# Passes of the expert value products reordered: by PSUM bank instead of by pass

## The chip, the cores and the metric

The kernel runs on one core of one Trainium2 chip. The metric is the device time of one execution in microseconds (us); lower is better. TensorE's clock has two levels here, 1.2 and 2.4 GHz; the profile shows the granted clock as a share of the higher one.

## The reference

One transformer-like layer (gated delta rule, mLSTM, a feed-forward part and a per-layer-embedding gate) is followed by a second block with two layers: an RG-LRU mixer and a forgetting-attention mixer, each followed by a PEER expert layer. There are 256 tokens (T) of width 1024 (D), all in float32. The change lies in the PEER layers:

```python
def retrieve_chunk(xc):
    ...
    expert = e1 * PEER_KEYS + e2
    g = jax.nn.softmax(top_s, axis=-1)
    u = jnp.take(expert_u, expert, axis=0)
    act = jax.nn.gelu(jnp.einsum('thkd,td->thk', u, xc).astype(jnp.float32), approximate=False)
    w = (g * act).astype(xc.dtype)
    return jnp.einsum('thk,thkd->td', w, jnp.take(expert_v, expert, axis=0))
```

There are 16384 experts, 128 x 128 keys. The kernel does not gather. It multiplies all experts and weights the unchosen ones with zero.

## The kernel before, in words

**Tiles.** Every weight matrix is streamed from HBM in tiles of 128 partitions x 1024 float32 (512 KB), through `ring`, which has 4 slots (`RAW`). SyncE issues these loads. A PEER layer (`experts(L)`, L = 0 and 1) streams 128 tiles of `expert_u` and then 128 tiles of `expert_v`, one tile for each first key.

**Three passes.** A float32 product is made of fp32r products. Each tile is cut into a high part (`high`, ScalarE, line 1645) and a low part, the tile minus its high part (`low`). GpSimd makes the low part of `expert_u` tiles (line 1766) and VectorE that of `expert_v` tiles (`values_low`, line 2312). Both `high` and `low` have 3 slots (`CUT`). The activations are cut likewise. A product is then high x high, high x low of the activations, and low x high: three passes, numbered 0, 1 and 2, and only pass 2 reads `low`.

**Stage hidden.** `hidden(s_)` multiplies one `expert_u` tile with the activations, 24 matmuls of 256 columns (3 passes x 8, line 1216), all into one bank of the PSUM tensor `mm`. Tile s_ takes bank s_ % 4. ScalarE applies gelu, VectorE weights the result (`weigh_hidden`, line 2295) into `placed`. Between hidden tiles stand the `place` groups (line 1237), which place the routing weights.

**Stage values.** `values(s_)` multiplies one `expert_v` tile (moving operand, two halves of 512 columns) with the weighted activations `wts` (stationary operand, 128 x 128, for the two token tiles c = 0 and 1). The four pairs of c and half have the four banks of the PSUM tensor `ms`, and each bank accumulates over all 128 tiles. A tile is 12 matmuls (line 1256). `wts` has 3 slots: its high part comes from ScalarE (`weights_high`, line 1674), its low part from VectorE (`weights_low`, line 2303), which raises `weighted`. In layer 0 the ring also carries 48 tiles of modulation weights during this stage, which VectorE adds up (lines 2325 and 2328).

**What sets the order.** Each engine's instructions stand in an order written out by hand, and semaphores join them. On TensorE `values(s_)` waits for `weighted` and `high_done`, and, ahead of its pass 2, for `low_done` (`low_ready(q)`, line 771). When its last matmul ends it raises `tiles_used`, which frees the slot of `high`, `low` and `wts` for the tile three later: ScalarE's cut of the high part waits for it. A slot of `ring` is freed by `low_done`. On VectorE the last hidden tile is weighted, then `weights_low` is made for the last slot, and then come `values_low(0)`, `(1)`, `(2)` and so on:

```python
for s_ in range(KEYS):
    values_low(s_)
    if s_ >= CUT:
        weights_low(s_)
```

After the 128th tile of a layer the four banks are copied out, turned by TensorE (line 1283) and added to `x`.

Of the kernel before, what the change touches and what calls it, by code (L numbers as in the profile page):

```python
# [31 lines left out]
TT = T // P  # L32
# [8 lines left out]
CUT = 3  # L41
# [389 lines left out]
def build(nc, streams, xT, pT, consts, vecs, small_w, fox_f_w, lru_gate_w, out):  # L431
    with ExitStack() as ctx:
        sem = Signals(nc, ctx)

        def sb(name, shape, dt=F32):
            return ctx.enter_context(nc.sbuf_tensor(name, shape, dt))
# [4 lines left out]
        high = sb("high", [P, CUT, SLOT], F32R)  # L441
        low = sb("low", [P, CUT, SLOT], F32R)
# [309 lines left out]
        def _(pe):  # L752
# [11 lines left out]
            def parts_of(name, i, width=SLOT):  # L764

                q = CUT0[name] + i
                pe.wait_ge(sem("high_done"), q + 1)
                return q, high[:, q % CUT, 0:width], low[:, q % CUT, 0:width]

            def low_ready(q):  # L770

                pe.wait_ge(sem("low_done"), q + 1)
# [176 lines left out]
            for u in range(8):  # L949
                hd, c = u // 2, u % 2  # L950
# [6 lines left out]
            for u in range(8):  # L957
                hd, c = u // 2, u % 2
# [14 lines left out]
            for u in range(8):  # L973
                hd, c = u // 2, u % 2
# [5 lines left out]
            for u in range(8):  # L980
                hd, c = u % 4, u // 4
# [119 lines left out]
            q, wh, wl = parts_of("w_out", 0)  # L1101
# [18 lines left out]
            for m in range(KD):  # L1120
                dst = bank(OUT0["ffn_down"] + m)[:, 0:T]
                k0 = 0
                for i, rows in enumerate(DOWN):
                    q, wh, wl = parts_of("ffn_down", 3 * m + i)
# [29 lines left out]
            for j in range(RT):  # L1154
                for b, kind in enumerate(("x", "g")):
                    q, wh, wl = parts_of("lru_in", 2 * j + b)
# [13 lines left out]
            for i, (m, half) in enumerate(LRU_OUT):  # L1170
# [3 lines left out]
                q, wh, wl = parts_of("lru_out", i)  # L1174
# [10 lines left out]
            def experts(L):  # L1185
# [56 lines left out]
                def values(s_):  # L1242

                    q = q0 + KEYS + s_
                    pe.wait_ge(sem("weighted"), KEYS * L + s_ + 1)
                    pe.wait_ge(sem("high_done"), q + 1)
                    if s_ == 0:
                        pe.wait_ge(sem("place_copied"), GROUPS * (L + 1))
                        pe.wait_ge(sem("place_weighed"), GROUPS * (L + 1))
                    for pass_, (a_, b_) in enumerate(((0, 0), (0, 1), (1, 0))):  # L1250
                        if pass_ == 2:
                            low_ready(q)
                        v_ = (high, low)[a_][:, q % CUT, :]
                        for c in range(TT):
                            for half in range(2):
                                ins_ = pe.matmul(ms[:, 2 * c + half, :], wts[:, s_ % 3, b_, c * P:(c + 1) * P],  # L1256
                                                 v_[:, half * 512:(half + 1) * 512], start=s_ == 0 and pass_ == 0,
                                                 stop=s_ == KEYS - 1 and pass_ == 2, skip_group_check=True)
                    ins_.then_inc(sem("tiles_used"), 1)
# [8 lines left out]
                for s_ in range(KEYS):  # L1268
                    values(s_)
                    if L == 0 and s_ in LATE_SUMS_AFTER:  # L1270
                        if s_ == LATE_SUMS_AFTER[0]:
                            pe.wait_ge(sem("hidden_weighed"), KEYS - FIRST_MIXED)
                        sum_late_mods([LATE_SUMS_AFTER.index(s_)], mm[:, 3])
# [3 lines left out]
                for b in range(4):  # L1277

                    c, half = b % 2, b // 2
# [1376 lines left out]
```

## Time and profile before

| | us |
|---|---|
| time, median of 3 runs | 2575.62 |
| lowest and highest run | 2573.45, 2577.27 |
| profiled execution, span from first to last instruction | 2581.3 |
| TensorE busy in it | 2480.5 (96%) |
| VectorE, ScalarE, GpSimd busy | 1757.1, 1224.5, 1210.8 |

The profiled execution's own device time is not listed beside its span; its span lies 5.7 us above the median of the runs. All times are us from the span's start. "PE" is TensorE's matmuls and "PEld" its weight loads; DVE is VectorE, ACT ScalarE, POOL GpSimd, SPq the DMA queue of SyncE. Matmuls are pipelined: a matmul starts while the one before it is still draining, so the time that a matmul takes of the engine is the distance between two starts, and not the mean duration of the row. The "chain" of the profile page is followed back from the last instruction through what released each step.

### The profile page before, as it was taken

What the parts mean: (1) busy time and instruction counts of PE and PEld (TensorE: products, weight loads), DVE (VectorE), ACT (ScalarE), POOL (GpSimd) and SP (SyncE); (2) the same over time, 40 slices, a digit from 0 to 9 for tenths busy, and PEclk for the clock granted to TensorE, in tenths of its full rate; (3) what the DMA queues carried; (4) which work ended last, traced back from release to release, by engine and by line L of the source; (5) the groups of instructions that cost most, each with busy time, mean ns of one, the idle gap of its engine ahead of it and who ended that gap; (6) DMA issues with size and microseconds to landing.
All of it is one profiled execution on the core that took longest, in us unless ns stands there. A gap on an engine that the chain in (4) does not pass through costs nothing.

```text
span 2581.3 us, 46939 instructions
## 1 busy us (share of the span) xinstructions
PE 2480.5 (96%) x18074; PEld 2294.0 (89%) x18074; DVE 1757.1 (68%) x3289; ACT 1224.5 (47%) x2091; POOL 1210.8 (47%) x506
## 2 busy tenths in 40 slices
PE   7899899979799999999999999999999999999999
PEld 6899899969789999998888888888999999888887
DVE  4558553367719979997776764651897999655555
ACT  5325433446445544444444444544555444445453
POOL 4437577645468987771000004446798777200000
PEclk8899899989899999999999998998999999999999
DMA  4325576754255655556777772334565445566664
GB/s 161 98 74 168 202 256 233 278 205 123 82 164 180 191 178 156 156 156 222 254 255 260 252 240 92 108 97 152 174 192 183 154 160 156 173 195 189 194 189 146
DMA packets 125918, 457.93 MB, mean 177 GB/s; under 512 B 13968, under 2 KB 15376, under 8 KB 125584
## 3 DMA queue, kind: packets, MB, share of 16 engines
q1 hardware_dynamic: 125424, 450.73, 54.5%
q10 hardware_dynamic: 288, 4.33, 0.4%
q8 instruction: 145, 2.38, 0.4%
q14 instruction: 61, 0.50, 0.1%
HBM read 453.95 MB, written 1.05 MB: 176 GB/s over the span
## 4 chain that ended last, share of the span: by engine, by line
PE 86%; DVE 7%; ACT 3%; issue 2%; DMA 1%; POOL 1%; SPq 0%; DVEq 0%; POOLq 0%; ACTq 0%
PE mm L1216 27%; PE ms L1256 27%; PE mm L786 20%; PE ms L1237 3%; PE ms L793 1%; DMA ring<-w_ple_gate 1%; DVE hs L1805 1%; PE mm L793 1%; PE mm L801 1%; DVE work L1805 1%; PE mm L899 1%; POOL low L1766 1%; DVE scratch L1805 1%; DVE work L2494 1%; DVE work L1799 0%
## 5 line engine op out<-in xcount | busy, mean ns | idle before, releaser
L1766 POOL TENSOR_TENSOR low<-ring,high 128x1024 fp32r<-128x1024 f32 (+2 forms) x502 | 1210.6, 2424 | 1004.4 <-ACT high L1438 847.2
L1645 ACT ACTIVATE high<-ring 128x1024 fp32r<-128x1024 f32 x506 | 536.3, 1060 | 356.4 <-PE ms L1256 320.3
L1216 PE MATMUL mm<-hs,high 128*128 128x256 f32 x4096 | 520.4, 280 | 3.4 <-ACT high L1438 3.4
L1256 PE MATMUL ms<-high,wts 128*128 128x512 f32 x2048 | 511.2, 392 | 0.0
L1216 PEld LDWEIGHTS mm<-hs,high 128*128 128x128 f32 x4096 | 486.8, 188 | 3.8 <-issue 3.8
L2312 DVE TENSOR_TENSOR low<-ring,high 128x1024 fp32r<-128x1024 f32 x256 | 313.5, 1226 | 248.3 <-ACT high L1645 248.0
L1256 PEld LDWEIGHTS ms<-high,wts 128*128 128x128 f32 x2048 | 384.2, 188 | 83.3
L786 PE MATMUL mm<-hs,high 128*128 128x256 f32 x2608 | 346.4, 287 | 4.8 <-DVE parts L1799 4.6
L1438 ACT ACTIVATE high<-ring 128x1024 fp32r<-128x1024 f32 (+2 forms) x252 | 258.1, 1031 | 185.4 <-PE mm L786 114.4
L786 PEld LDWEIGHTS mm<-hs,high 128*128 128x128 f32 x2608 | 326.0, 196 | 9.3 <-issue 7.7
L1256 PE MATMUL ms<-low,wts 128*128 128x512 f32 x1024 | 275.7, 391 | 3.0 <-DVE low L2312 3.0
L1216 PE MATMUL mm<-hs,low 128*128 128x256 f32 x2048 | 274.0, 276 | 0.5 <-POOL low L1766 0.5
L1216 PEld LDWEIGHTS mm<-hs,low 128*128 128x128 f32 x2048 | 251.1, 188 | 0.9 <-POOL low L1766 0.9
L1256 PEld LDWEIGHTS ms<-low,wts 128*128 128x128 f32 x1024 | 192.1, 188 | 46.2 <-DVE low L2312 3.8
L786 PE MATMUL mm<-hs,low 128*128 128x256 f32 x1304 | 178.1, 279 | 0.4 <-POOL low L1766 0.4
L1653 ACT ACTIVATE mm<-mm 128x256 f32<-128x256 f32 (+47 forms) x148 | 39.7, 268 | 269.8 <-PE mm L1216 269.8
L786 PEld LDWEIGHTS mm<-hs,low 128*128 128x128 f32 x1304 | 163.6, 191 | 0.7 <-POOL low L1766 0.6
L2277 DVE TENSOR_TENSOR onehots<-onehots,ms 128x512 bf16<-128x512 bf16 x256 | 163.3, 679 | 0.0
L1447 ACT ACTIVATE work<-mm 128x256 f32<-128x256 f32 (+2 forms) x145 | 60.2, 417 | 205.6 <-PE mm L786 168.2
L1655 ACT ACTIVATE work<-mm 128x256 f32<-128x256 f32 (+17 forms) x248 | 79.9, 322 | 137.1 <-PE mm L1216 137.1
L786 PE MATMUL mm<-parts,high 128*128 128x256 f32 x896 | 126.9, 294 | 15.7 <-DVE parts L1799 10.2
L786 PEld LDWEIGHTS mm<-parts,high 128*128 128x128 f32 x896 | 117.1, 199 | 18.4 <-DVE parts L1799 10.7
(315 smaller groups left out, 2802.3 us busy)
## 6 DMA issues: line engine op xcount, KB each, us to landing
ring<-w_peer_experts SPq DMA_DIRECT2D x512, 512.0 KB, 3.7
work<-w_mod SPq DMA_DIRECT2D x48, 512.0 KB, 4.5
ring<-w_late_mods SPq DMA_DIRECT2D x48, 512.0 KB, 4.6
ring<-w_ffn_up SPq DMA_DIRECT2D x44, 512.0 KB, 3.7
ring<-w_peer_q SPq DMA_DIRECT2D x32, 512.0 KB, 3.6
ring<-w_fox_in SPq DMA_DIRECT2D x32, 512.0 KB, 3.6
ring<-w_lru_in SPq DMA_DIRECT2D x22, 512.0 KB, 3.5
ring<-w_gates SPq DMA_DIRECT2D x16, 512.0 KB, 3.6
```

The lines of the kernel that those rows point to most:

```text
L786: ins = pe.matmul(dst, l, r_, start=first and s_ == 0 and k == 0, stop=last and s_ == 2 and k == rows - 1, skip_group_check=True)
L1216: ins_ = pe.matmul(mm[:, s_ % BANKS, 0:T], w_[:, k * P:(k + 1) * P], hs[:, b_, k, :], start=pass_ == 0 and k == 0, stop=pass_ == 2 and k = ...
L1237: ins_ = pe.matmul(ms[:, 2 + i % 2, t * P:(t + 1) * P], onehot[:, i % 2, 3, t, :], onehot[:, i % 2, third, t, :], start=third == 0, stop=t ...
L1256: ins_ = pe.matmul(ms[:, 2 * c + half, :], wts[:, s_ % 3, b_, c * P:(c + 1) * P], v_[:, half * 512:(half + 1) * 512], start=s_ == 0 and pa ...
L1438: act.activation(high[0:rows, q % CUT, 0:width], ring[0:rows, n_ % RAW, 0:width], ACT.Copy) \
L1447: S.did(act.activation(dst, src, func), taken(n))
L1645: act.activation(high[:, (q0 + i) % CUT, :], ring[:, n_ % RAW, :], ACT.Copy) \
L1655: ins = act.activation(placed[:, s_, at:T], src[:, at:T], ACT.Gelu)
L1766: pool.tensor_tensor(low[0:rows, cut_slot, 0:width], ring[0:rows, raw_slot, 0:width], high[0:rows, cut_slot, 0:width].bitcast(F32), ALU.su ...
L1805: S.did(dve.scalar_tensor_tensor(out=out_, in0=a, scalar=s, in1=b, op0=op0, op1=op1, **kw), name)
L2277: dve.tensor_tensor(onehot[:, k % 2, s], onehot[:, k % 2, 2], third(s), ALU.mult)
L2312: dve.tensor_tensor(low[:, q % CUT, :], ring[:, n % RAW, :], high[:, q % CUT, :].bitcast(F32), ALU.subtract).then_inc(sem("low_done"), 1)
```

## The change

`low_ready(q)` is called ahead of the tile's first matmul, and the loops are turned inside out. Before, a pass went over all four banks and then the next pass did; now each bank gets its three passes, one behind the other. The 12 matmuls of a tile, their operands, and the flags `start` and `stop` of each are the same, and so are all other engines' instructions (one line of code fewer moves the line numbers behind it by one).

```diff
-                    for pass_, (a_, b_) in enumerate(((0, 0), (0, 1), (1, 0))):
-                        if pass_ == 2:
-                            low_ready(q)
-                        v_ = (high, low)[a_][:, q % CUT, :]
-                        for c in range(TT):
-                            for half in range(2):
+                    low_ready(q)
+                    for c in range(TT):
+                        for half in range(2):
+                            for pass_, (a_, b_) in enumerate(((0, 0), (0, 1), (1, 0))):
+                                v_ = (high, low)[a_][:, q % CUT, :]
                                 ins_ = pe.matmul(ms[:, 2 * c + half, :], wts[:, s_ % 3, b_, c * P:(c + 1) * P],
                                                  v_[:, half * 512:(half + 1) * 512], start=s_ == 0 and pass_ == 0,
                                                  stop=s_ == KEYS - 1 and pass_ == 2, skip_group_check=True)
```

TensorE, from the end of the last hidden tile of layer 0 into value tile 0, before (output, then operands, then partitions x columns):

```order
L1216 MATMUL mm<-hs,low 128x256 [waits low_done]
L1216 MATMUL mm<-hs,low 128x256 x7
L1256 MATMUL ms<-high,wts 128x512 [waits place_copied,place_weighed,high_done,weighted]
L1256 MATMUL ms<-high,wts 128x512 x7
L1256 MATMUL ms<-low,wts 128x512 [waits low_done]
L1256 MATMUL ms<-low,wts 128x512 x3
L1256 MATMUL ms<-high,wts 128x512 [waits high_done,weighted]
```

The same place after the change:

```order
L1216 MATMUL mm<-hs,low 128x256 [waits low_done]
L1216 MATMUL mm<-hs,low 128x256 x7
L1255 MATMUL ms<-high,wts 128x512 [waits place_weighed,place_copied,low_done,high_done,weighted]
L1255 MATMUL ms<-high,wts 128x512
L1255 MATMUL ms<-low,wts 128x512
L1255 MATMUL ms<-high,wts 128x512 x2
L1255 MATMUL ms<-low,wts 128x512
L1255 MATMUL ms<-high,wts 128x512 x2
L1255 MATMUL ms<-low,wts 128x512
L1255 MATMUL ms<-high,wts 128x512 x2
L1255 MATMUL ms<-low,wts 128x512
L1255 MATMUL ms<-high,wts 128x512 [waits low_done,high_done,weighted]
```

The wait for the low part has moved over eight matmuls, from the ninth to the first, and now joins the others there.

TensorE, a later value tile of layer 0 (tile 1), before:

```order
L1256 MATMUL ms<-high,wts 128x512 [waits high_done,weighted]
L1256 MATMUL ms<-high,wts 128x512 x7
L1256 MATMUL ms<-low,wts 128x512 [waits low_done]
L1256 MATMUL ms<-low,wts 128x512 x3
L1256 MATMUL ms<-high,wts 128x512 [waits high_done,weighted]
```

And after the change:

```order
L1255 MATMUL ms<-high,wts 128x512 [waits low_done,high_done,weighted]
L1255 MATMUL ms<-high,wts 128x512
L1255 MATMUL ms<-low,wts 128x512
L1255 MATMUL ms<-high,wts 128x512 x2
L1255 MATMUL ms<-low,wts 128x512
L1255 MATMUL ms<-high,wts 128x512 x2
L1255 MATMUL ms<-low,wts 128x512
L1255 MATMUL ms<-high,wts 128x512 x2
L1255 MATMUL ms<-low,wts 128x512
L1255 MATMUL ms<-high,wts 128x512 [waits low_done,high_done,weighted]
```

In every tile the low products now stand third, sixth, ninth and twelfth, and a tile has one place to wait instead of two.

## Rows read from the trace of the kernel before

**Rows 1.** Page, part 4: the chain that ended last, shares of the span by line
```profile
PE mm L1216 27%; PE ms L1256 27%; PE mm L786 20%; PE ms L1237 3%; PE ms L793 1%; DMA ring<-w_ple_gate 1%; DVE hs L1805 1%; PE mm L793 1%; PE mm L801 1%; DVE work L1805 1%; PE mm L899 1%; POOL low L1766 1%; DVE scratch L1805 1%; DVE work L2494 1%; DVE work L1799 0%
```

**Rows 2.** Page, part 5: matmul groups of the value products; count, busy, mean ns, idle
```profile
L1256 PE MATMUL ms<-high,wts 128*128 128x512 f32 x2048 | 511.2, 392 | 0.0
...
L1256 PE MATMUL ms<-low,wts 128*128 128x512 f32 x1024 | 275.7, 391 | 3.0 <-DVE low L2312 3.0
```

**Rows 3.** Timeline, TensorE, value tile 0 of layer 0: start, us, count, idle before
```profile
1182.38 2.00 PE L1256 MATMUL ms<-high,wts 128*128 128x512 f32 x8
1185.86 1.19 PE L1256 MATMUL ms<-low,wts 128*128 128x512 f32 x4 [1.49 <-DVE low L2312]
1186.89 2.00 PE L1256 MATMUL ms<-high,wts 128*128 128x512 f32 x8
```

**Rows 4.** Timeline, ScalarE and VectorE in that stretch, and VectorE's cut of tile 3
```profile
1183.81 0.41 ACT L1674 ACTIVATE wts<-work 128x256 fp32r<-128x256 f32 x1
1184.25 0.42 DVE L2303 TENSOR_TENSOR wts<-work,wts 128x256 fp32r<-128x256 f32 x1 [0.77 <-ACT wts L1674]
1184.59 3.49 DVE L2312 TENSOR_TENSOR low<-ring,high 128x1024 fp32r<-128x1024 f32 x3
...
1190.57 1.23 DVE L2312 TENSOR_TENSOR low<-ring,high 128x1024 fp32r<-128x1024 f32 x1 [1.82 <-ACT high L1645]
```

**Rows 5.** Timeline, TensorE, value tile 0 of layer 1
```profile
2219.58 2.00 PE L1256 MATMUL ms<-high,wts 128*128 128x512 f32 x8
...
2223.06 1.19 PE L1256 MATMUL ms<-low,wts 128*128 128x512 f32 x4 [1.48 <-DVE low L2312]
```

**Rows 6.** Timeline, layer 1: the parts of value tile 3, and its start
```profile
2225.45 1.23 DVE L2312 TENSOR_TENSOR low<-ring,high 128x1024 fp32r<-128x1024 f32 x1 [0.16 <-ACT high L1645]
...
2226.59 0.42 DVE L2303 TENSOR_TENSOR wts<-work,wts 128x256 fp32r<-128x256 f32 x1
...
2229.58 2.00 PE L1256 MATMUL ms<-high,wts 128*128 128x512 f32 x8
```

**Rows 7.** Timeline, TensorE, from hidden tile to hidden tile
```profile
1176.03 1.07 PE L1216 MATMUL mm<-hs,low 128*128 128x256 f32 x8
1176.94 1.98 PE L1216 MATMUL mm<-hs,high 128*128 128x256 f32 x16
1178.75 1.07 PE L1216 MATMUL mm<-hs,low 128*128 128x256 f32 x8
```

**Rows 8.** Windows: busy (count) by engine, granted clock, DMA share, GB/s
```profile
336.00:341.00 5.00, 5.00 (x24) 5.00 (x25) 3.33 (x5) 1.11 (x2) 2.38 (x1) 0.50 0.60 205
...
693.50:696.90 3.40, 3.40 (x19) 3.40 (x18) 0.00 (x0) 0.88 (x3) 3.06 (x2) 0.50 0.35 110
...
1182.00:1190.00 8.00, 6.51 (x31) 5.13 (x31) 4.92 (x6) 2.16 (x4) 0.00 (x0) 1.00 0.38 121
...
2224.00:2572.00 348.00, 348.00 (x1522) 285.51 (x1521) 196.59 (x252) 170.57 (x250) 0.00 (x0) 1.00 0.60 188
```

**Rows 9.** Timeline, TensorE, behind an idle stretch of 4.58 us
```profile
335.90 3.75 PE L786 MATMUL mm<-hs,high 128*128 128x256 f32 x16 [4.58 <-DVE parts L1799]
339.45 1.91 PE L786 MATMUL mm<-hs,low 128*128 128x256 f32 x8
341.15 2.36 PE L786 MATMUL mm<-hs,high 128*128 128x256 f32 x16
343.35 1.07 PE L786 MATMUL mm<-hs,low 128*128 128x256 f32 x8
```

**Rows 10.** Timeline, TensorE, behind an idle stretch of 2.53 us
```profile
692.21 2.69 PE L786 MATMUL mm<-parts,high 128*128 128x256 f32 x16 [2.53 <-DVE x L1805]
694.70 1.91 PE L786 MATMUL mm<-parts,low 128*128 128x256 f32 x8
696.41 1.10 PE L786 MATMUL mm<-parts,high 128*128 128x256 f32 x6
697.35 0.52 PE L786 MATMUL mm<-parts,low 128*128 128x256 f32 x3
```

## The prediction

> **What bounds the kernel now.** I read the page first: the chain that ended last runs over TensorE, with 27% of the span in the value products and 27% in the hidden ones [rows 1]. So a nanosecond saved or lost on each value matmul counts in full, and so does a microsecond in which TensorE stands still in that stage. The groups by line then give the size of the stage and its one fault: 2048 + 1024 = 3072 matmuls, with 3.0 us idle ahead of the low products, released by VectorE's cut of the low part [rows 2]. The timeline finds the 3.0 us: 1.49 us in tile 0 of layer 0 [rows 3] and 1.48 us in tile 0 of layer 1 [rows 5]. Everywhere else the stage is dense: from 2224 to 2572 us TensorE is busy for the whole 348 us, with 1522 matmuls and the clock at its upper level [rows 8], which is 348 / 1522 = 228.7 ns from start to start. The row's mean duration of 392 ns is not what a matmul takes of the engine.
>
> **The change, part by part.** The 3072 matmuls and as many weight loads stay. Two things move: the wait for the low part, eight matmuls forward, and the order of the banks.
>
> *The wait, in the steady state: nothing.* For tile 3 of layer 1 the low part is ready at 2225.45 + 1.23 = 2226.68, and the low part of `wts`, for which the tile's first matmul waits in any case, only at 2226.59 + 0.42 = 2227.01; the tile starts at 2229.58 [rows 6]. The new wait thus ends 0.33 us ahead of one that stands there already, and 2.9 us ahead of its use. What hides it is the tile that runs meanwhile, 12 x 0.229 = 2.75 us. If that cover were gone, the price would be the 1.83 us of the eight matmuls, in each of 256 tiles, but nothing here takes it away: ScalarE starts to cut a tile when the tile three before it is done, and has two tiles' time. Layer 0 is tighter, as the ring also carries the modulation tiles: its tile 3 has its low part at 1190.57 + 1.23 = 1191.80 [rows 4] and starts at 1186.89 + 2 x 2.75 = 1192.39, 0.6 us later. That still suffices, and the later start of tile 0 (below) adds 1.8 us to it.
>
> *The wait, in tile 0 of each layer: 1.83 us.* In layer 0 the low part is made from 1184.59 on, behind the last `wts` parts on ScalarE and VectorE (to 1184.22 and 1184.67) [rows 4]; they come from the last hidden tile, and nothing of that chain depends on a value product. So it is ready at the same moment as before, and TensorE resumes at 1185.86 [rows 3]. Before, eight matmuls had run by then (from 1182.38 on) and four were left. Now all twelve are left. The eight cost 8 x 228.7 ns = 1.83 us on the chain. Layer 1 shows the same stretch: start at 2219.58, resumed at 2223.06 [rows 5]. Two layers: 2 x 1.83 = 3.7 us. It is not won back, since the stage behind is bound by TensorE itself. Tiles 1 and 2 are not late: VectorE makes three low parts in one stretch of 3.49 us, the last ready at 1188.1 [rows 4], and tile 1 now starts at 1186.89 + 1.83 = 1188.7. Queued behind the waiting TensorE is only its own stream; ScalarE's cut for tile 3 waits for the end of tile 0, and moves by 1.8 us along with it, within the 2.9 us of slack.
>
> *The clock behind the longer gap: 2.3 us a layer.* Now TensorE has no matmul between the last hidden one and the resumption. A group of eight such matmuls is busy for 0.16 us beyond the start of the next group (1176.03 + 1.07 against 1176.94) [rows 7], so the last hidden one ends at 1182.38 + 0.16 = 1182.54, and the idle stretch is 1185.86 - 1182.54 = 3.3 us, where it was 1.49. The stretch of 1.49 us left the clock at 1.00 [rows 8]. How a longer one is answered, two places show. Behind 2.53 us idle the clock fell to 0.50 (1.2 GHz) from 693.5 to 696.9 [rows 8], and 16 + 8 + 6 = 30 matmuls took 697.35 - 692.21 = 5.14 us [rows 10]; at 0.113 us each, the distance at the upper level [rows 7], they take 3.40. That is 1.7 us lost. Behind 4.58 us idle it was 0.50 as well [rows 8], and 40 matmuls took 343.35 - 335.90 = 7.45 us in place of 4.53 [rows 9], 2.9 us lost. My 3.3 us lies between these two, so I take the middle, 2.3 us, with 1.7 and 2.9 as ends, and zero as the outer bound if the clock doesn't fall. Two layers: 4.6 us.
>
> *The order of the banks: nothing.* Before, every value matmul went to another bank than the one ahead of it; now only four of twelve do. The trace has no value matmul that stays in its bank. The nearest rows are the hidden tiles, which stay in one bank for 24 matmuls and then change it. The eight low matmuls that end a tile, the change of bank, of tile and of pass included, take 1176.94 - 1176.03 = 0.91 us, or 114 ns each, and the 16 within a tile 1178.75 - 1176.94 = 1.81 us, or 113 ns each [rows 7]. So neither staying nor changing has a price at 256 columns, within the 10 ns to which the rows are given. I take zero for 512 columns. The bounds: in its own bank a 256-column matmul takes 113.3 ns for 256 columns, which is 226.7 ns for 512, and the value matmul takes 228.7. If the whole difference of 2.0 ns came from changing banks, 8 x 256 = 2048 matmuls would give back 4.1 us. The other bound: 113.3 ns is 6.6 ns above the 106.7 ns that 256 columns take at 2.4 GHz, and 228.7 is 15.4 ns above 213.3 ns; if 6.6 ns is fixed and the other 8.8 ns is the bank, 2048 x 8.8 ns = 18.0 us. I stay near zero since rows 7 see the very event and show no price. Upwards I allow 2 ns as well (+4.1 us), as staying in a bank might cost what changing does.
>
> *Weight loads: nothing.* The old order used each stationary tile twice in a row, the new one changes it at nearly every matmul. Each matmul has its own load in both, and the loads lie beside the matmuls: busy 285.51 of 348 us with no matmul idle [rows 8].
>
> **The sum.** 3.7 + 4.6 = 8.3 us. Against the profiled execution: 2581.3 + 8.3 = 2589.6. That execution's span lies 5.7 us above the median of the runs, 2575.6, and the difference carries over: 2575.6 + 8.3 = 2583.9 us, 0.32% slower. About 0.2%, 5.2 us, is what a measurement of this kernel can tell from no change.
>
> **The rivals.**
> 1. *The clock holds in both layers.* Then 3.7 us remain: 2579.3, within 0.2%. For it: 1.49 us idle did nothing. Against it: the idle stretch of 2.53 us did. If it falls in one layer alone, it is 3.7 + 2.3 = 6.0, 2581.6 us, just on the slower side.
> 2. *Changing banks had a price at 512 columns, and TensorE gets faster.* Its place is the steady state of both value stages. Each nanosecond is worth 2.05 us, so 4.1 ns pays for the sum, and 6.6 ns makes the kernel faster by over 0.2%. With the 8.8 ns from above it is 2575.6 + 8.3 - 18.0 = 2565.9 us. For it: 15.4 ns above the column time want an explanation. Against it: rows 7, and the clock at 1.00 and no idle through the 348 us [rows 8].
> The Trainium skill's page "TensorE: Matmul & The Clock Gate", section "A second HAM failure mode: psum-queue depth-cycling", speaks for this rival: it tells of a kernel with 512-column matmuls which lost throughput as it cycled through the banks, with TensorE idle between groups and its clock swinging. The trace disagrees, as there is neither idle time nor a lower clock to give back here. The same page, "Back-to-back issue gap", gives about 216 ns for an isolated 512-column matmul; as an estimate by that figure, a value matmul freed of all its surplus over it would give 2048 x 12.7 ns = 26 us, more than my bound from rows.
> 3. *Staying in a bank costs.* A write that must add to what the one just before it left may have to wait. At 5 ns that is 10 us more, 2594 us. Against it: the hidden tiles do just this, at 113 ns.
> 4. *The change does nothing that counts.* The low part might come earlier by some freed time elsewhere, and the order of TensorE's stream is certain. That leaves 2575.6. I see no engine that gets anything freed ahead of tile 0.
>
> **How the numbers follow.** Forecast (clock falls in both layers, banks free): 0.60. One layer alone: 0.12. Clock holds: 0.11. Banks gain: 0.08, of which half ends within 0.2% (the small bound: 8.3 - 4.1 = +4.2) and half faster. Staying costs: 0.04. Nothing: 0.05. Slower by over 0.2% are the forecast, the costly bank and most of the one-layer case (0.04 of its 0.12 falls back within the measurement's spread): 0.60 + 0.04 + 0.08 = 0.72, less 0.03 for runs that come out low, 0.69. Faster: 0.04, and 0.01 of spread, 0.05. Within 0.2%: the rest, 0.26. The range: its upper end is the sum with both clocks at their end, 3.7 + 5.8 = 9.5, and half the spread of the runs, 1.9, so 2587; its lower end the clock that holds, 2579.3, less the same 1.9 and rounded down, 2577. Left out are the banks' large gain, the costly bank and nothing at all, under 2 in 10.
>
> **What would show it.** Idle time ahead of the value matmuls of about 3.3 us twice, in the first tile, released by VectorE's low part, and none elsewhere. A granted clock of 0.50 in the microseconds behind 1186 and 2225. Tile 1 1.8 us later against the last hidden matmul, and more with the clock. From there on 228.7 ns from start to start and 2.75 us a tile. If that distance is another one, the bank step is wrong; if the low wait shows in later tiles, the slack is; if the clock stays at 1.00, the clock step is.

## The result and the profile after

| | before | after |
|---|---|---|
| time, median of 4 runs, us | 2576.11 | 2592.45 |
| lowest and highest run, us | 2573.45, 2577.27 | 2587.87, 2599.67 |
| ratio, 95% interval | | 1.0053 [1.0036, 1.0069] |
| profiled execution, span, us | 2581.3 | 2597.9 |

The changed kernel is slower, by 16.3 us in this comparison. 8.3 were forecast, and 2592.45 lies above the range, which ended at 2587.0. Three of the four runs of the kernel before are the three from which the forecast was made. The profiled execution of the changed kernel took 2599.67 us, 1.8 us more than its span of 2597.9.

The page of the changed kernel, part 4 (shares of the span by line) and the groups of the value products in part 5, which answer to [rows 1, 2]:

```profile
PE ms L1255 27%; PE mm L1216 27%; PE mm L786 20%; PE ms L1237 3%; PE ms L793 1%; DMA ring<-w_ple_gate 1%; PE mm L793 1%; DVE hs L1804 1%; DVE work L1804 1%; PE mm L899 1%; PE mm L801 1%; POOL low L1765 1%; DVE scratch L1804 1%; DVE work L2493 1%; DVE work L1798 0%
...
L1255 PE MATMUL ms<-high,wts 128*128 128x512 f32 x2048 | 638.4, 393 | 6.8 <-DVE low L2311 6.8
...
L1255 PE MATMUL ms<-low,wts 128*128 128x512 f32 x1024 | 404.3, 395 | 0.0
```

The idle time has grown from 3.0 to 6.8 us, has moved from the low products to the high ones, and is still released by VectorE's low part. The busy times of the two groups (511.2 and 275.7 us before) look 256 us larger. That is no loss: since high and low products now alternate, each group also counts the time in which the other one's pipelined matmul is draining. The counts of matmuls in fixed windows tell better. Here are the changed kernel's (busy and count by engine, then granted clock, DMA share, GB/s):

```profile
1193.00:1200.00 7.00, 6.29 (x15) 4.97 (x16) 3.50 (x4) 0.74 (x1) 0.00 (x0) 0.51 0.75 239
1203.00:1210.00 7.00, 7.00 (x32) 5.73 (x31) 5.35 (x6) 3.48 (x6) 0.00 (x0) 1.00 0.63 193
2234.00:2241.00 7.00, 5.82 (x14) 4.59 (x15) 3.30 (x3) 0.27 (x1) 0.00 (x0) 0.51 0.61 208
2260.00:2560.00 300.00, 300.00 (x1313) 246.14 (x1312) 170.26 (x219) 149.52 (x219) 0.00 (x0) 1.00 0.62 191
```

From 2260 to 2560 us 1313 value matmuls ran, as against 1312 in the same 300 us of the kernel before:

```profile
2260.00:2560.00 300.00, 300.00 (x1312) 246.15 (x1311) 170.31 (x218) 149.29 (x219) 0.00 (x0) 1.00 0.62 191
```

So the order of the banks changed nothing there. What did change is at the start of each value stage, where the clock stands at half (0.51 is a window that lies almost wholly at 1.2 GHz). Layer 0, TensorE, in the changed kernel (start, us, count, idle before), which answers to [rows 3]:

```profile
1189.23 1.07 PE L1216 MATMUL mm<-hs,low 128*128 128x256 f32 x8
1193.71 1.19 PE L1255 MATMUL ms<-high,wts 128*128 128x512 f32 x2 [3.41 <-DVE low L2311]
1194.70 0.63 PE L1255 MATMUL ms<-low,wts 128*128 128x512 f32 x1
1195.12 1.05 PE L1255 MATMUL ms<-high,wts 128*128 128x512 f32 x2
...
1198.96 1.03 PE L1255 MATMUL ms<-high,wts 128*128 128x512 f32 x2
```

TensorE stands idle for 3.41 us. Then a bank's three matmuls take 1195.12 - 1193.71 = 1.41 us, 0.43 to 0.56 us each, and the twelve of tile 0 take 1198.96 - 1193.71 = 5.25 us, where 2.75 was the time at the upper clock. From the last hidden matmul to the last value matmul of the stage it took 365.15 us in layer 0 and 357.76 in layer 1, read off the starts in the timeline; before, it was 360.44 and 353.22. That is 4.71 + 4.54 = 9.25 us in the places which the change touches. The two spans differ by 16.6 us. The other 7.3 us lie in code that the change leaves alone. They lie ahead of the first value tile, which starts 11.3 us later (1193.71 against 1182.38), 3.6 of them by its own wait.

### The profile page after: what moved, and what is told of

Same layout as the page of the kernel before. It is cut to its first block, busy times and chain, and to the rows that moved or that the text cites. A ratio compares the mean times of both kernels' runs of the same rounds, so it can differ in the third digit from the quotient of the medians.

```text
span 2597.9 us, 46939 instructions
## 1 busy us (share of the span) xinstructions
PE 2492.5 (96%) x18074; PEld 2305.9 (89%) x18074; DVE 1750.2 (67%) x3289; ACT 1225.0 (47%) x2091; POOL 1210.6 (47%) x506
## 4 chain that ended last, share of the span: by engine, by line
PE 86%; DVE 7%; ACT 3%; issue 2%; DMA 1%; POOL 1%; SPq 0%; DVEq 0%; POOLq 0%; ACTq 0%
PE ms L1255 27%; PE mm L1216 27%; PE mm L786 20%; PE ms L1237 3%; PE ms L793 1%; DMA ring<-w_ple_gate 1%; PE mm L793 1%; DVE hs L1804 1%; DVE work L1804 1%; PE mm L899 1%; PE mm L801 1%; POOL low L1765 1%; DVE scratch L1804 1%; DVE work L2493 1%; DVE work L1798 0%
## 5 line engine op out<-in xcount | busy, mean ns | idle before, releaser
L1255 PE MATMUL ms<-high,wts 128*128 128x512 f32 x2048 | 638.4, 393 | 6.8 <-DVE low L2311 6.8
L1255 PE MATMUL ms<-low,wts 128*128 128x512 f32 x1024 | 404.3, 395 | 0.0
```

## The experiments

### The same kernels again, and each half of the change alone

The first four ran together. Two are unchanged copies. The third moves the wait alone:

```diff
+                    low_ready(q)
                     for pass_, (a_, b_) in enumerate(((0, 0), (0, 1), (1, 0))):
-                        if pass_ == 2:
-                            low_ready(q)
                         v_ = (high, low)[a_][:, q % CUT, :]
```

The fourth has the order by banks in every tile but the first of each layer:

```diff
+                    if s_ == 0:
+                        for pass_, (a_, b_) in enumerate(((0, 0), (0, 1), (1, 0))):
+                            if pass_ == 2:
+                                low_ready(q)
...
+                    else:
+                        low_ready(q)
+                        for c in range(TT):
+                            for half in range(2):
+                                for pass_, (a_, b_) in enumerate(((0, 0), (0, 1), (1, 0))):
...
```

> The kernel before, unchanged, as a control: 2576 us in every theory, within 0.1% of its own runs. What it tells is the spread: in the profiled executions the 256-column matmuls stand at either of two distances at the upper clock, 113.3 or 117.8 ns, for stretches of tens to hundreds of us (the profile of before has 11 us above 113.3 ns in all, that of after 21 us). Theory LUCK: the level is drawn anew in each execution, so the control has executions with 15 to 20 us of it too, and single runs 5 us or more above the others. Theory PROGRAM: the level depends on the program, and the control repeats 2573 to 2578 us.

> The changed kernel again, in more rounds. Theory START (the longer wait in tile 0 of each layer and the half clock behind it, 3.95 to 4.6 us a layer in the traces): 9 us over before, 2585 us, and the rest of the 16 us was chance. Theory PROGRAM or BANK: 2592 us again, 16 us over before, and the 7 us more lie outside tile 0 of the layers.

> Only the wait for the low part is moved ahead of the tile's first matmul; the order of the banks is that of before. Theory START: the whole loss is here, 9 us (2 x 1.83 for the eight matmuls, and 2 x 2 to 2.9 for the clock), 2585 us. Theory BANK: 9 us here, and the after kernel another 7 us above this one. Theory PROGRAM: 16 us here as well, as in after.

> The order by banks in tiles 1 to 127 of each layer, while tile 0 keeps the order by passes with its wait ahead of the ninth matmul. Theory START: 2576 us, no difference, and no half clock at the start of the value stages. Theory BANK: 7 us over before, with a larger distance between the value matmuls. Theory PROGRAM: some us over before, with the 256-column matmuls ahead of the value stages at 117.8 ns for longer than in before.

| | runs | median, us | lowest, highest | ratio to before, interval |
|---|---|---|---|---|
| before, beside them | 34 | 2582.74 | 2573.11, 2589.86 | |
| before again | 12 | 2583.80 | 2575.65, 2591.39 | 0.9999 [0.9982, 1.0015] |
| after again | 11 | 2593.89 | 2588.40, 2602.24 | 1.0049 [1.0032, 1.0066] |
| wait alone | 12 | 2589.99 | 2583.88, 2599.47 | 1.0035 [1.0018, 1.0052] |
| banks alone | 12 | 2584.91 | 2577.57, 2594.86 | 1.0013 [0.9995, 1.0031] |

**The control.** The kernel before does not repeat within 4 us. Its 34 runs spread over 17 us, with a median of 2582.7. The three runs that the forecast started from all lie below that. The two profiled executions of this program show one thing that differs. Both windows are from 800 to 900 us, in the hidden stage of layer 0, first in the kernel before as profiled at the outset:

```profile
800.00:900.00 100.00, 100.00 (x885) 100.00 (x884) 98.83 (x278) 53.22 (x78) 96.99 (x38) 1.00 0.63 194
```

and then in the control, the same program:

```profile
800.00:900.00 100.00, 100.00 (x851) 100.00 (x851) 98.37 (x285) 51.84 (x76) 93.36 (x36) 1.00 0.60 185
```

TensorE is busy throughout and the clock is at its upper level in both, yet 885 matmuls of 256 columns ran in the one and 851 in the other: 113.0 and 117.5 ns apart. So the distance differs from execution to execution, as LUCK had it; PROGRAM can't make one program differ from itself. These two alone don't show that it makes the spread, as their spans are 2581.3 and 2581.8 us.

All 14 profiled executions together say more. Without the stretches of the next table their spans differ by up to 14.6 us. In that remainder the matmuls at the slower distance add 3.4 us in one execution and up to 14.8 in another, and with this subtracted the executions differ by up to 6.5 us. (Counted from the traces as groups of eight 256-column matmuls, in lines 786 and 1216, that stand 2.5 to 6.5 ns each above 113.3 ns.) So it goes with the larger part of the spread there; what makes the rest was not found. In the profile of the changed kernel it adds 14.8 us and in that of the kernel before 4.6, more than the 7.3 us by which the two differ outside the value stages. Those 7.3 us are thus no effect of the change that any run shows.

**The halves.** The traces of the start and the rest of the value stages can be compared to a hundredth of a us, without the spread of the whole. Time from the last hidden matmul to the last value matmul of each layer, read off the timelines, in us:

| profiled execution | layer 0 | layer 1 | both, over before | half clock behind the gap |
|---|---|---|---|---|
| before | 360.44 | 353.22 | | none |
| before again | 360.42 | 353.22 | -0.02 | none |
| after | 365.15 | 357.76 | +9.25 | 6.8 and 6.8 |
| after again | 366.71 | 356.71 | +9.76 | 6.8 and 3.4 |
| wait alone | 363.91 | 356.70 | +6.95 | 3.4 and 3.4 |
| banks alone | 360.71 | 353.51 | +0.56 | none |

The time of "after again", 11.2 us above before with an interval of 8 to 17 us, does not choose between the 9 us of START and the 16 of the others. The stages do: they hold 9.76 us.

Wait alone carries the loss. Its ratio of 1.0035 is 9 us, and its interval, 5 to 13 us, leaves out the 16 of PROGRAM. In the timeline of its layer 1 TensorE is idle for the same 3.41 us ahead of tile 0, and tile 0 takes 2227.40 - 2222.98 = 4.42 us:

```profile
2218.51 1.07 PE L1216 MATMUL mm<-hs,low 128*128 128x256 f32 x8
2222.98 3.12 PE L1255 MATMUL ms<-high,wts 128*128 128x512 f32 x8 [3.41 <-DVE low L2311]
2225.90 1.66 PE L1255 MATMUL ms<-low,wts 128*128 128x512 f32 x4
2227.40 1.99 PE L1255 MATMUL ms<-high,wts 128*128 128x512 f32 x8
```

Banks alone costs 0.28 us a layer. I take it for a wait and no cost of the banks: tile 1 now waits for its low part at its first matmul, and VectorE makes that part (3.49 - 1.23) / 2 = 1.13 us behind that of tile 0 [rows 4], while the four matmuls left of tile 0 last 0.92. The kernels with early low parts below, in which this order costs nothing, bear that out. The ratio of 1.0013 leaves open anything from -0.05 to 0.31%. Whether there is more in it, the next experiments had to tell.

### Fill the gap, or remove the reason for it

The next four ran together on another chip. In the first, TensorE does 14 useless matmuls (3.2 us of work) while it waits; the products that follow overwrite them:

```diff
+                    if s_ == 0:
+                        for f_ in range(14):
+                            pe.matmul(ms[:, f_ % 4, :], wts[:, 0, f_ % 2, 0:P], high[:, q % CUT, 0:512],
+                                      start=True, stop=True, skip_group_check=True)
                     low_ready(q)
```

In the second and third, VectorE makes the low parts of value tiles 0 and 1 earlier. The second has the order by passes, the third the order by banks:

```diff
                         if groups_before(k):
                             weigh_hidden(k)
+                        if k >= KEYS - 2:
+                            values_low(k - KEYS + 2)
                         if k >= KEYS - 3:
                             weights_low(k - KEYS + 3)
                 for s_ in range(KEYS):
-                    values_low(s_)
+                    if s_ >= 2:
+                        values_low(s_)
```

> The changed kernel, with 14 more matmuls of 512 columns in tile 0 of each layer, ahead of its wait for the low part. Their results are overwritten by the tile's first products; they only fill the idle 3.5 us with 14 x 0.229 = 3.2 us of work. Theory START splits the loss into the wait (1.83 us a layer) and what the idle stretch does to TensorE's clock and spacing; the filling leaves the wait and takes the other part away: 3.7 us over before, no half clock behind the last hidden tile, tile 1 at 6.5 us behind the last hidden matmul in both layers (4.63 before, 8.1 to 8.9 after the change). If the idle stretch costs nothing of its own, it is as slow as after, 11 to 13 us over before.

> The kernel before, with the low parts of value tiles 0 and 1 made on VectorE behind hidden tiles 126 and 127, where it is idle, rather than behind all the weights parts. Theory START: TensorE's stall of 1.6 us in tile 0 goes in both layers, tile 1 starts 2.86 us behind the last hidden matmul in place of 4.63, and the kernel is 2 x 1.77 = 3.5 us faster than before. If another wait takes its place (the weights' low part of tile 2, which now stands behind a low part), some of it comes back.

> The changed kernel with the same early low parts. Theory START: with the low part there in time, the order by banks has nothing to wait for, and the kernel is equal to the one with early low parts and the order by passes: 3.5 us faster than before, 16 us faster than after. Theory BANK: it stays 3 us above that kernel, as the kernel with the banks' order in tiles 1 to 127 alone stood 3 us (mean, of an uncertainty as large) above its control.

> The changed kernel once more, beside the three others. 11 to 13 us over before again. In the profile: half clock for 3.4 or 6.8 us behind the last hidden tile, in both layers. Theory LUCK adds: value tiles behind it stand at 2.75 or at 2.80 us, drawn anew behind the idle stretch, where before they always stood at 2.75; one of six such stages in the three profiles so far had 2.80.

| | runs | median, us | ratio to before, interval | stages over before, us |
|---|---|---|---|---|
| before, beside them | 35 | 2578.44 | | |
| gap filled | 12 | 2580.99 | 1.0006 [0.9994, 1.0018] | +3.64 |
| low parts early, by passes | 12 | 2575.28 | 0.9983 [0.9972, 0.9994] | -3.54 |
| low parts early, by banks | 12 | 2575.54 | 0.9983 [0.9971, 0.9994] | -3.54 |
| after, third time | 12 | 2590.86 | 1.0043 [1.0027, 1.0059] | +14.54 |

(The last column is the same measure as in the table above, from each one's profiled execution.)

**Filled.** TensorE in layer 0 of the kernel with the filled gap:

```profile
1174.86 1.07 PE L1216 MATMUL mm<-hs,low 128*128 128x256 f32 x8
1175.77 3.37 PE L1252 MATMUL ms<-high,wts 128*128 128x512 f32 x14
1179.25 0.73 PE L1259 MATMUL ms<-high,wts 128*128 128x512 f32 x2
```

and its windows behind the last hidden tile, in both layers:

```profile
1179.00:1190.00 11.00, 10.89 (x48) 8.85 (x48) 7.30 (x9) 4.10 (x6) 0.00 (x0) 1.00 0.75 262
2217.00:2228.00 11.00, 10.89 (x48) 8.64 (x47) 6.64 (x8) 4.10 (x6) 0.00 (x0) 1.00 0.63 206
```

The clock stays at 1.00, and what is left is 3.64 us for both layers. That is 1.82 us a layer, where the forecast had 1.83 for the eight matmuls. More work made the changed kernel faster: 0.06% over before in place of 0.43%. The Trainium skill's page "TensorE: Matmul & The Clock Gate", in its table "Why this matters for your kernels", advises against idle gaps between bursts of matmuls; these two traces, which differ by the filling alone, show the case.

**Early.** With the low parts made early there is nothing to wait for, in either order. TensorE in layer 1, with the order by banks:

```profile
2217.33 1.07 PE L1216 MATMUL mm<-hs,low 128*128 128x256 f32 x8
2218.24 0.62 PE L1255 MATMUL ms<-high,wts 128*128 128x512 f32 x2
2218.69 0.39 PE L1255 MATMUL ms<-low,wts 128*128 128x512 f32 x1
2218.92 0.62 PE L1255 MATMUL ms<-high,wts 128*128 128x512 f32 x2
```

The low products follow without a gap, and a bank's three matmuls take 2218.92 - 2218.24 = 0.68 us, 0.23 each. The two kernels with early low parts are equal: the same ratio, and stages that agree to 0.01 us. The 300 us from 2260 to 2560 have the same count in both to within one matmul, by passes

```profile
2260.00:2560.00 300.00, 300.00 (x1312) 246.15 (x1312) 170.56 (x219) 149.65 (x220) 0.00 (x0) 1.00 0.61 189
```

and by banks

```profile
2260.00:2560.00 300.00, 300.00 (x1313) 246.12 (x1312) 170.18 (x218) 149.67 (x219) 0.00 (x0) 1.00 0.61 189
```

That settles BANK: the order of the banks is free here, at 512 columns too. The 228.7 ns that a value matmul takes don't come from changing banks; what they do come from was not looked for. Both kernels beat both of the case, the kernel before by 0.17% and the changed one by about 0.6%.

### What sets the distance of the matmuls behind the half clock

In the third profile of the changed kernel layer 1 was 6.8 us longer than with the same half clock elsewhere. Its window at full clock:

```profile
2260.00:2560.00 300.00, 300.00 (x1287) 242.99 (x1286) 167.41 (x215) 146.26 (x214) 0.00 (x0) 1.00 0.60 188
```

There are 1287 matmuls in place of 1313, 233.1 ns apart in place of 228.5. The second profile had it in layer 0, for 1.6 us. So the slower distance seen in the hidden stage exists for 512 columns as well. Four more executions, single runs on a third chip, were to tell whether the gap brings it on.

> A look at the changed kernel, for its profile alone. Theory REDRAW: behind the half clock at the start of a value stage the distance of the matmuls is drawn between 228.8 ns (2.75 us a tile) and 233.3 ns (2.80 us); so far 2 of 8 such stages had 2.80, and none of 12 stages without a half clock. Of the 8 stages of these four looks 1 to 4 have 2.80. Theory OTHER: the 2.80 has to do with something else, and none of the 8 shows it.

> As the look before this one, a second execution of the changed kernel.

> A look at the kernel with the wait alone moved, for its profile: half clock in both layers as in after; REDRAW expects 2.80 us tiles here as often as with the order by banks (1 in 4), OTHER, by the order of the banks, never.

> As the look before this one, a second execution of the kernel with the wait alone moved.

The times were 2592.37 and 2593.66 us (after) and 2586.68 and 2588.52 us (wait alone), beside one run of before at 2583.36. None of the eight stages showed 2.80 us a tile. Over before, the stages took 8.16, 8.20, 9.31 and 9.29 us. Altogether 2 of 16 stages with a half clock had the slower distance, and 0 of 12 without one. That is against my expectation of 1 to 4 in these eight, and too few to call the link shown. It stays open. In the hidden stages, which the change leaves alone, the slower distance came in 6 of 28, for about 145 us each, once of these in the kernel before. The half clock itself is settled: it came in all 16 stages with the gap, for 3.4 us in six of them and for 6.8 us in ten, in the order by passes as well as by banks.

## Why the prediction was right or wrong

**Right.** The bound (TensorE in the value stage) and the place of the loss (tile 0 of each layer, twice, and no later tile). *The wait in the steady state: nothing*: no other tile of the value stages has idle time released by VectorE. *The wait in tile 0*: 1.83 us a layer forecast, 1.82 measured with the gap filled. The idle stretch: 3.3 us forecast, 3.41 measured. *The clock behind the longer gap*: it fell in every one of the 16 stages, in both layers. Its size, 2.3 us a layer, was right as well. With 1.82 us taken off for the wait, and the slower distance where it came, the ten stages of the five profiles of the changed kernel lost 1.4 to 2.9 us to it, 2.3 in the mean. In layer 0 of the first of them, 6.8 us at half clock cost 4.71 - 1.82 = 2.9 us; in layer 1 of the second, 3.4 us cost 3.49 - 1.82 = 1.7. The forecast took the middle of these two ends and had no ground for their weights. The long one came in six of the ten, so that the mean fell there is in part luck. *The order of the banks: nothing*: shown by the two kernels with early low parts. The two places of the trace that stood for it, the distance within a hidden tile and over its end [rows 7], were enough to read it from. What the Trainium skill's page "TensorE: Matmul & The Clock Gate", section "A second HAM failure mode: psum-queue depth-cycling", tells of a kernel that lost throughput as it cycled through banks, with idle time between its groups, does not bear on this stream: with early low parts the clock was at 1.00 and the distance the same in both orders.

**Wrong.** The time lay 5.5 us above the range. Two steps of the prediction failed, and neither is the mechanism of the change.

The first is *the sum's base* and the room for chance around it: "That execution's span lies 5.7 us above the median of the runs, 2575.6, and the difference carries over". The three runs, within 3.8 us of each other, were taken for the kernel's spread, and the range had 1.9 us for it. The control's 46 runs on one chip spread over 18 us, with medians of 2582.7 and 2583.8, and the 35 on another had 2578.4. From such a base, 2578 to 2583, the sum of 8.3 us gives 2587 to 2591, against medians of 2590.9 to 2593.9. The profile had a sign of it which I did not read. An execution's time is 1.8 us more than its span where both are known, so the profiled execution of before took about 2583.1 us (an estimate), 5.8 above the highest of the three runs. It was not an execution with something added, but another draw. The sum put on it, the 2589.6 us of the prediction, is a span, or 2591.4 us of time, which is 1.1 short of the measured 2592.45.

The second is a term that the prediction put at nothing without a reason: the distance of the matmuls at the upper clock was to be the same in both ("From there on 228.7 ns from start to start"). The runs showed two distances. In the value stages of the changed kernel the slower one added 1.6 and 6.8 us in two of ten, 1.7 us an execution in the mean. In the profiles of the first comparison it added 10.2 us more after than before in code that the change leaves alone.

The sum itself came out: the stages of the five profiles of the changed kernel took 9.25, 9.76, 14.54, 8.16 and 8.20 us more, 10.0 in the mean, and 8.3 without the slower distance, where 8.3 were forecast.

Against the larger comparisons the forecast of the difference was 8.3 us, or 0.32%, where 0.49% [0.32, 0.66] and 0.43% [0.27, 0.59] were measured. The trace accounts for 10.0 of these 11 to 13 us. The rest, 1 to 3 us, is within the intervals and not explained. The 16.3 us of the first comparison are in part chance: its four runs of before, three of them those of the forecast, were all lower than the median of either later set.

## What to carry to other kernels

A wait that is moved ahead of independent work costs that work only where the thing waited for is late, so look for it at the start of each stage and not in the steady state; there it also joins two short idle stretches or lengthens one, and the longer one can cost the clock on top, here as much again as the wait. If such a gap can't be closed by making its cause earlier on an idle engine, work that is thrown away can be cheaper than idling, as it was here. And three runs that agree are no measure of the spread of a kernel: before a change of 0.3% is priced against them, an unchanged copy should be run beside it.

## What the hardware showed that was not expected

With the clock at its upper level and TensorE never idle, the same matmuls stand at one of two distances, 113.0 or 117.5 ns at 256 columns and 228.5 or 233.1 ns at 512: 4.5 ns more each, whatever their length. In these stages the slower one held for 80 to 350 us, and in the same instructions of the same program it differed between executions (885 and 851 matmuls in the same 100 us). In all seven places where it ended within a stage, matmuls of another shape had come in between, with no idle time and no change of the clock. In "after again" it was 233 ns up to 1279.63 us, where matmuls of one column (line 892) come in, and less behind them:

```profile
1200.00:1270.00 70.00, 70.00 (x301) 56.72 (x301) 49.25 (x60) 34.15 (x51) 0.00 (x0) 1.00 0.80 254
1290.00:1360.00 70.00, 70.00 (x316) 57.76 (x315) 48.92 (x59) 34.12 (x50) 0.00 (x0) 1.00 0.79 257
```

In the 14 profiled executions it went with the larger part of the spread outside the value stages. What picks the one or the other was not found.
